# Expert layer of a fused float32 block: routing steps, row fetches and routing matrices placed four to seven units earlier in a hand-written order

## The reference, cut to what matters

```
q = (xb @ wq).reshape(128, 8, 2, 64)
s1, s2 = dot products of q with 128 keys each, per head
v1, i1 = top_k(s1, 16); v2, i2 = top_k(s2, 16)
sc, ci = top_k(v1[..., None] + v2[..., None, :], 16)
e = i1[ci // 16] * 128 + i2[ci % 16]
g = softmax(sc)
hid = einsum('thkd,td->thk', u[e], xb)
return einsum('thk,thkd->td', gelu(hid) * g, v[e])
```

## Time and profile before

| | us |
|---|---|
| median of 3 runs | 3089.75 |
| lowest and highest | 3089.43, 3090.46 |
| the profiled execution | 3089.17 |
| its span | 3087.4 |

### The profile page before, as it was taken

How to read it: one execution, slowest core, us unless ns; L and a number is a source line. 1 busy time by engine, 2 the same in 40 slices (tenths; PEclk the granted TensorE clock), 3 DMA queues, 4 the chain that set the end, 5 groups by cost and what they waited for, 6 DMA issues and landing times.

```text
span 3087.4 us, 42622 instructions
## 1 busy us (share of the span) xinstructions
PE 3053.1 (99%) x15287; PEld 2583.2 (84%) x15287; DVE 1847.6 (60%) x3298; ACT 1149.4 (37%) x2064; POOL 1899.4 (62%) x1796
## 2 busy tenths in 40 slices
PE   8999999999999999999999999999999999999999
PEld 6877788888668888888777888999999998888887
DVE  7674444315856442250673236688878868877885
ACT  3465322102553221120554212434467763333333
POOL 7432666677337666776433576588875566766662
PEclk9999999999999999999999999999999999999999
DMA  7210222222212222222112222488888899999995
GB/s 229 75 41 29 96 102 97 96 96 101 77 42 103 96 96 96 96 103 96 69 55 76 78 95 99 172 289 292 299 314 319 326 350 371 367 364 358 364 363 202
DMA packets 153709, 539.26 MB, mean 175 GB/s; under 512 B 11155, under 2 KB 64564, under 8 KB 117172
## 3 DMA queue, kind: packets, MB, share of 16 engines
q1 hardware_dynamic: 97296, 334.78, 30.5%
q0 software_dynamic: 36864, 134.23, 12.0%
q10 hardware_dynamic: 19364, 67.72, 5.8%
HBM read 479.16 MB, written 57.40 MB: 174 GB/s over the span
## 4 chain that ended last, share of the span: by engine, by line
PE 97%; DVE 2%; issue 1%; ACT 0%; DMA 0%; ACTq 0%; DVEq 0%
PE banks L194 85%; PE banks L2850 3%; PE banks L2191 1%; PE banks L2229 1%; PE banks L1127 1%; PE banks L1214 1%; PE banks L1186 1%; PE banks L2208 1%; PE banks L1196 1%; PE banks L2794 1%; PE banks L1752 0%; PE banks L1790 0%; PE banks L1768 0%; PE banks L1712 0%; DVE memory L573 0%
## 5 line engine op out<-in xcount | busy, mean ns | idle before, releaser
L194 PE MATMUL banks<-memory,weights_split 128*128 128x512 f32 (+1 forms) x9456 | 2066.7, 376 | 14.1 <-DVE memory L573 10.7
L194 PEld LDWEIGHTS banks<-memory,weights_split 128*128 128x128 f32 x9456 | 1713.5, 188 | 288.1 <-issue 34.8
L3426 POOL TENSOR_SCALAR weights_split<-weights_raw 128x512 fp32r<-128x512 f32 x576 | 375.8, 662 | 775.6 <-PE banks L194 387.2
L3431 POOL TENSOR_TENSOR weights_split<-weights_raw,weights_split 128x512 fp32r<-128x512 f32 x576 | 768.9, 1347 | 0.0
L3292 POOL TENSOR_TENSOR weights_split<-weights_raw,weights_split 128x512 fp32r<-128x512 f32 x384 | 505.4, 1340 | 311.5 <-ACT weights_split L3134 309.5
L194 PE MATMUL banks<-weights_split,memory 128*128 128x512 f32 (+1 forms) x2880 | 646.4, 386 | 0.0
L194 PEld LDWEIGHTS banks<-weights_split,memory 128*128 128x128 f32 x2880 | 533.6, 188 | 108.9 <-issue 1.0
L3134 ACT ACTIVATE weights_split<-weights_raw 128x1024 fp32r<-128x1024 f32 x256 | 269.4, 1053 | 81.4 <-DMA weights_raw<-in_weights 39.9
L707 DVE TENSOR_TENSOR banks<-banks,memory 128x512 f32<-128x512 f32 x88 | 61.3, 699 | 231.9 <-PE banks L194 231.8
L2922 DVE CUSTOM_DVE_ANT_0 memory<-memory,banks 128x1024 f32<-128x1024 f32 x128 | 155.0, 1212 | 68.4 <-DMA memory<-in_peer_u,memory 68.3
L3286 POOL DMA_INDIRECT memory<-in_peer_v,memory x128 | 154.8, 1209 | 44.3 <-issue 24.4
(11 more groups left out here) (280 smaller groups left out, 2724.9 us busy)
## 6 DMA issues: line engine op xcount, KB each, us to landing
weights_raw<-in_weights SPq DMA_DIRECT2D x272, 1024.0 KB
routing<-memory ACTq DMA_DIRECT2D x12, 2048.0 KB
hidden<-memory ACTq DMA_DIRECT2D x62, 384.0 KB
memory<-hidden SPq DMA_DIRECT2D x31, 768.0 KB
memory<-routing SPq DMA_DIRECT2D x30, 768.0 KB
window_rows<-memory ACTq DMA_DIRECT2D x1, 3064.0 KB, 26.7
chunk_rows<-memory ACTq DMA_DIRECT2D x1, 2556.0 KB, 12.4
residual<-in_x ACTq DMA_DIRECT2D x4, 512.0 KB, 8.5
```

The lines of the kernel that those rows point to most:

```text
L194: last = k.nc.tensor.matmul(out, left[a], right[b], start=start and n == 0, stop=stop and n == 2, skip_group_check=True)
L3426: k.nc.gpsimd.tensor_scalar(cut(high, n * PIECE, PIECE), cut(raw, n * PIECE, PIECE), 1.0, 1.0, ALU.mult, ALU.mult).then_inc(k.high_made, 1)
L3431: k.nc.gpsimd.tensor_tensor(cut(low, n * PIECE, PIECE), cut(raw, n * PIECE, PIECE), cut(high, n * PIECE, PIECE).bitcast(F32), ALU.subtract ...
```

## The change

The positions are moved towards the layer's first unit, and the fetches with them. No instruction is added or removed.

```
-    SCORE_AT, EXP_AT, TURN_AT = [0, 8, 27, 50], [15, 38, 60, 82], [None, 45, 67, 84]
-    MATRIX_FIRST, MATRIX_COUNT = 85, 34
+    SCORE_AT, EXP_AT, TURN_AT = [0, 8, 20, 46], [10, 34, 56, 78], [None, 41, 63, 80]
+    MATRIX_FIRST, MATRIX_COUNT = 81, 34
...
-        marks = [(19, 0), (42, 22), (64, 44), (84, 66), (118, 116), (125, DOTS), (PEER_KEYS + 3, DOTS),
+        marks = [(10, 0), (38, 22), (60, 44), (80, 66), (114, 112), (124, DOTS), (PEER_KEYS + 3, DOTS),
                  (PEER_KEYS + SPARSE_END, 2 * DOTS)]
...
-                goal = planned(unit - 3) + ahead if unit > 20 else 0
+                goal = planned(unit - 3) + ahead if unit > 13 else 0
```

## The result

| us | before | the change |
|---|---|---|
| median of 11 runs | 3089.78 | 3098.02 |
| lowest and highest | 3088.50, 3090.60 | 3094.62, 3101.19 |
| profiled execution, span | 3089.17, 3087.4 | 3095.24, 3093.4 |

The ratio is 1.0026, 95% interval 1.0018 to 1.0034: slower by some 8 us, outside the predicted range. The runs also lie 6.6 us apart where they lay 2.1 apart before. The profiled execution is one of the faster ones of the change; its span is 6.0 us longer.

A forecast was written before the change was run, and what follows sets the result against it. TensorE, busy for 1173.87 of the layer's 1174.30 us, was taken as the bound. Profiled 3089.17 + 0 + 0 + 0 = 3089.2 us; against the runs' median 3089.75, unchanged at 3089.8 was predicted, range 3088.6 to 3092.8.

The forecast's parts named there:

- TensorE bounds the layer and nothing can be won: Expert layer: matmuls cover 1173.87 of 1174.30 us, so at most 0.43 us to win; other engines' waits are no profit.
- First exponentials, first fetches: First routing: exponentials done at 1966.0, VectorE begins block 1 at 1973.1; first fetch 1972.2, first dot 1984.9.
- The tightest place, unit 26: Row 12's fetch waits for row 11's dot; low part ends 2032.4, TensorE wants it 2033.5: margin 1.1 us, cost 0.
- Later routings: Blocks 1 to 3: block 1's margin over 20 us, the last block's 2.5; no cost.
- Routing matrices: Fetch lead shrinks from six rows to two; only row 115 matters; possible TensorE wait 3.1 us, taken as 0.
- The end: Units behind the last matrices: first gates ready 2555.1, TensorE wants them 2558.7, margin 3.6 us, should not shrink.
- The rival that was right in place: One of two thin margins overdrawn, TensorE waits 0.5 to 3 us, 3090.3 to 3092.8 us; chance 0.06.
- The slower rival: Before unit 26's low part GpSimd waits for row 11's dot, 7.3 us late: 3096 us or more; chance 0.04.

The follow-up runs named there:

- The versions with the lead given back: Changed kernel with 116 or 114 rows planned by unit 114, not 112: 3089.28, 3089.67 us; or fetches nine rows ahead from unit 90, not six: 3089.14 us.
- The last experiment: Changed kernel with 116 rows put back and 22 rows planned by unit 34, not 38: median 3096.77 us, ratio 1.0023.
- half of the step: Changed kernel with 114 rows planned by unit 114, half way between 112 and 116: median 3089.67 us, ratio 1.0000.
- the second: Second profile, from the changed kernel run again with no edit: median 3099.96 us, ratio 1.0035, profiled span 3095.0 us.

## Why the prediction was wrong

*TensorE bounds the layer and nothing can be won*: right. The versions with the lead given back, 3089.1 to 3089.7, stand where the kernel before does, the first routing's 15 us of VectorE gained or not.

*First exponentials, first fetches*: right. L3024 does not wait, block 1 begins at 1973.42 (1973.1 predicted), the first dot at 1985.11 (1984.9); the first fetch is at 1972.81 (1972.2), since L3019 took 1.1 us, not 0.2.

*The tightest place, unit 26*: right, to a microsecond. In the changed kernel's timeline of GpSimd:

```profile
2028.13 0.95 POOL L3286 DMA_INDIRECT memory<-in_peer_u,memory  x1 [6.31 <-DVE memory L2922]
2029.11 2.54 POOL L3292 TENSOR_TENSOR weights_split<-weights_raw,weights_split 128x512 fp32r<-128x512 f32 x2
```

2028.9 and 7 us were predicted; the low part ends at 2031.65, and TensorE, in 20 units from 2012.56 without a break, begins unit 26 at 2033.4: margin 1.8 for 1.1. Row 11's dot began at 2026.64, not 2027.4. The prediction had both L3003 and L3004 held for 1.33 us; in the change L3003 took 1.31 us, from 2020.60, and L3004 only 0.21, since unit 25's low part had ended at 2021.82. The last experiment shows what an overdrawn margin would have cost.

*Later routings*: right; TensorE turns the last choices at 2263.21, where unit 80 was due, with no wait.

*Routing matrices*: **the step that failed**. It said that "only the last of them matters: row 115", took 6.2 us from fetch to dot, bounded it by "the longest that I find", 9.7, which would have cost 3.1, and took that wait as 0, because the 9.7 came from another stretch. TensorE waited twice, 2.05 and 2.29 us, and lost 6.2. Three things were wrong in the step.

First the size of a row's way. Row 115 took 8.9 us, well within the 9.7 that was set aside. Its fetch is 4.7 us into unit 113, so by the step's own arithmetic it can be used 6.6 us into unit 114, where 4.1 was wanted: 2.5 late, and TensorE waited 2.29. Row 110 took 13.3 us, beyond the bound. The trace of before held such ways, though none of them among the matrices, where no row from 78 to 117 was waited for and the way doesn't show: this pair, of GpSimd's timeline and VectorE's, is row 121 of the kernel before, right behind the matrices, 15.5 us with a wait at its end.

```profile
2514.88 0.94 POOL L3286 DMA_INDIRECT memory<-in_peer_u,memory  x1 [0.31 <-issue]
...
2530.41 1.22 DVE L2922 CUSTOM_DVE_ANT_0 memory<-memory,banks 128x1024 f32<-128x1024 f32 x1 [4.02 <-DMA memory<-in_peer_u,memory]
```

I had looked at one pair near the end and at the first of all, and called one of them the longest. With 13.3 the same arithmetic gives the first wait: row 110's fetch is 6.0 us into unit 109 (2458.28), usable at 2477.6, wanted at 2475.3 (unit 111's start at 2471.21, plus 6.0, less 1.9): 2.3 late, and TensorE waited 2.05.

Second, which rows matter. Not only the last: each row whose dot stands right ahead of a `weigh_rows` whose group is the third of its unit. From unit 110 on there are three, rows 110, 113 and 115. VectorE stood 3.3 us for row 113 as well, but TensorE, held up at group 86 before, came to group 92 only as it was ready: `weigh_rows` began at 2494.08 and took 0.7, and TensorE wanted it at 2495.1. Where TensorE had not stood before (half of the stores left out) it waited for just this group.

Third, a wait is not paid once. The first carried 1.4 us at half clock behind it. And ScalarE copies TensorE's matrices ahead of its split of the next weights, and GpSimd fetches behind the low part, so TensorE's wait puts off the fetches of the rows that come next; GpSimd's low part behind the first wait came after 5.84 us of idleness, the one ahead of it after 3.17, and the next rows behind it. That the loss feeds itself like this is argued from the order and these rows; no run takes this loop alone. It isn't needed for a later wait either: with half of the stores left out TensorE stood for row 113's group with no stop before it. Why rows took between 6 and 13 us in the same stretch stays open.

*The end*: as predicted in kind. The gates wait for their transfer and are ready at 2561.2, TensorE wants them at 2564.76: margin 3.6, as before.

The rival that was right in place, small waits at a thin margin, was wrong in size: 0.5 to 3 us against 8 in the median, 5 to 11 in single runs. The slower rival's margin was sound, and never overdrawn by this change.

## What to carry to other kernels

When a change makes a prefetch leaner, measure the lead where it is leanest, in us from issue to use, against the longest way in the trace, and take that from all issues whose user waited at their end, not from one or two. Count the lead up to where the user is ready, not up to where it starts, since its wait is in the latter. Here leads of 11.0 us and more cost nothing, and leads of 3.7 to 10.9 cost 8 us of the median; half of the step cost nothing and the whole of it 8, so a check by halves says little about the next half.

Where one engine is never idle, as TensorE here, another engine's slack is worth nothing until it is gone. VectorE then stood 19.2 us for rows, of which only what TensorE had to stand for was paid, 4.3 us, and the clock's share on top.

## What the runs showed of the hardware that I had not expected

After idle spells of 2.05, 2.06 and 3.83 us TensorE had a stretch at half clock, and the next unit took 5.6 to 5.9 us for 4.25. After 5.06 us it lost some 2.7 us in this way. After the 2.29 us of the first profile it lost nothing, after the 1.89 us of the second it lost 1.0. The length of the idle spell alone does not tell which it will be. The runs of the change spread over 6.6 us.

Of two rows that GpSimd asks for 1.25 us apart, the second took far longer: 8.6 and 13.3 us for rows 109 and 110, 7.0 and 12.1 for rows 113 and 114, each with VectorE waiting at its end. It is not always so: row 117, asked for 1.26 us behind row 116, was there within 6.2 us, as row 116 was.
